# Recurrence of a streaming encoder on one core: each set of transposes placed behind a gate unit of its own

## What is computed

```python
p = hn @ w_in                                   # q, fp, vi, z: 8 heads x 128 columns each
f = lb + (1 - lb) * sigmoid(fp); q = silu(q); g = log(f); k = 1 - f; v = vi
b = cumsum(g)                                   # within a chunk
o = einsum(scores(q, k, b), v) + (q * exp(b)) @ S0
S = exp(b_last) * S0 + (k * exp(b_last - b)).T @ v
o = o * rsqrt(mean(o * o) + EPS) * gnorm        # per head
out = (o * silu(z)) @ w_out
```

## Time and profile before

| what | value |
|---|---|
| device time, median of 3 runs | 1507.84 us (1505.77 to 1508.29) |
| profiled execution, its own time | 1508.62 us |
| its span, first to last instruction | 1506.8 us |
| mean granted TensorE clock | 0.979 of full speed |
| busy share | PE 93%, PEld 81%, DVE 62%, ACT 43%, POOL 37% |

### The profile page before, as it was taken

The page is one execution under the profiler, slowest core; times in us unless marked ns, Lnnn a source line. Parts: engine busy times, 40 slices in busy tenths (PEclk is TensorE's granted clock), DMA queues, the critical chain, the costliest instruction groups (busy, mean ns, idle before and its releaser), DMA issues. The chain is left out here.

```text
span 1506.8 us, 21428 instructions
## 1 busy us (share of the span) xinstructions
PE 1404.7 (93%) x8109; PEld 1220.5 (81%) x8109; DVE 933.7 (62%) x1765; ACT 643.4 (43%) x1136; POOL 559.2 (37%) x402
## 2 busy tenths in 40 slices
PE   4999999999996899999988999999999999998898
PEld 3999746999995455548878998989999999997786
DVE  7111388787793989744556676667676757576333
ACT  6233464677664555541122625243434343443121
POOL 4276501265553001100012646465555556464000
PEclk9999999999998999999998999999999999999899
DMA  6112100232312410001231101010101111105221
GB/s 223 29 43 57 28 1 15 72 87 75 96 48 67 140 29 15 4 24 63 100 88 43 43 20 57 20 57 20 57 27 50 35 43 34 43 6 201 99 85 63
DMA packets 96181, 86.79 MB, mean 58 GB/s; under 512 B 4528, under 2 KB 84272, under 8 KB 96080
## 3 DMA queue, kind: packets, MB, share of 16 engines
q1 hardware_dynamic: 94448, 80.60, 17.3%
q0 software_dynamic: 1632, 4.82, 0.9%
HBM read 65.43 MB, written 19.97 MB: 57 GB/s over the span
## 5 line engine op out<-in xcount | busy, mean ns | idle before, releaser
L186 PE MATMUL bank<-hn_hi,rw_hi 128*128 128x352 f32 x768 | 250.8, 327 | 1.5 <-PEq L1059 1.5
L186 PE MATMUL bank<-hn_hi,rw_lo 128*128 128x352 f32 x768 | 247.6, 322 | 0.0
L186 PE MATMUL bank<-hn_lo,rw_hi 128*128 128x352 f32 x768 | 247.3, 322 | 0.0
L186 PE MATMUL bank<-hn_hi,w_hi 128*128 128x352 f32 x672 | 218.9, 326 | 3.6 <-PEq L274 3.6
L186 PE MATMUL bank<-hn_lo,w_hi 128*128 128x352 f32 x672 | 216.4, 322 | 0.0
L186 PE MATMUL bank<-hn_hi,w_lo 128*128 128x352 f32 x672 | 216.2, 322 | 0.0
L186 PEld LDWEIGHTS bank<-hn_hi,rw_hi 128*128 128x128 f32 x768 | 144.9, 189 | 3.4 <-issue 3.0
L186 PEld LDWEIGHTS bank<-hn_lo,rw_hi 128*128 128x128 f32 x768 | 145.3, 189 | 0.0
L186 PEld LDWEIGHTS bank<-hn_hi,rw_lo 128*128 128x128 f32 x768 | 144.9, 189 | 0.0
L186 PEld LDWEIGHTS bank<-hn_hi,w_hi 128*128 128x128 f32 x672 | 126.9, 189 | 4.3 <-issue 3.7
L186 PEld LDWEIGHTS bank<-hn_lo,w_hi 128*128 128x128 f32 x672 | 127.2, 189 | 0.0
(11 more groups left out here) (233 smaller groups left out, 2950.5 us busy)
## 6 DMA issues: line engine op xcount, KB each, us to landing
rw_raw<-in_rec_w_in SPq DMA_DIRECT2D x32, 512.0 KB, 4.0
w_raw<-in_att_w_in SPq DMA_DIRECT2D x30, 512.0 KB, 4.0
q_rotated<-relu SPq DMA_DIRECT2D x24, 176.0 KB, 1.9
xin<-in_x_prompt SPq DMA_DIRECT2D x8, 512.0 KB, 4.1
q_tile<-q_rotated SPq DMA_DIRECT2D x8, 512.0 KB, 3.7
wo_raw<-in_att_w_out SPq DMA_DIRECT2D x4, 1024.0 KB, 10.0
x_again<-in_x_prompt SPq DMA_DIRECT2D x8, 512.0 KB, 4.1
residual<-h_rows SPq DMA_DIRECT2D x8, 512.0 KB, 2.9
```

What stands on the lines that cost most here:

```text
L186: last = pe.matmul(out, l, r, start=n == 0, stop=n == len(passes) - 1)
```

## The change

The value transposes of a head stood behind its value units (unit 8), and the output transposes of the head before and the key transposes together behind unit 11. Now the value transposes stand behind unit 9, the output transposes of the head before behind unit 10, the key transposes behind unit 11. On ACT the read of unit 9 stands ahead of the copy of the value transposes, with its wait for `zT` to be free. No instruction is added or taken away, and no other engine's list changes.

```diff
@@ PE, loop over heads p @@
                 for j in range(3, 9):
                     project(u + j)
+                project(u + 9)
                 for g in range(3):
                     multiply("v_T", p, g)
-                for j in range(9, 12):
-                    project(u + j)
+                project(u + 10)
                 if p:
                     for g in range(3):
                         multiply("out_T", p - 1, g)
+                project(u + 11)
                 for g in range(3):
                     multiply("k_T", p, g)
@@ ACT, loop over heads p @@
                 for j in range(5, 9):
                     decay(p, j)
+                if p >= 2:
+                    act.wait_ge(dve_read, n_dve[at["out_T", p - 2, 2, None] + 1])
+                read_projection(u + 9)
                 for g in range(3):
                     read_product("v_T", p, g, v[:, p % 2])
-                if p >= 2:
-                    act.wait_ge(dve_read, n_dve[at["out_T", p - 2, 2, None] + 1])
-                for j in range(9, 12):
+                for j in range(10, 12):
                     read_projection(u + j)
                 split(4 * p + 3 + SLOTS)
```

## The result

The changed kernel takes 1514.43 us in the median of 5 runs (1513.08 to 1515.18), the kernel before 1508.29 us beside it (1505.77 to 1509.12). The ratio is 1.0043, with a 95% interval of 1.0028 to 1.0058: slower by 6.1 us, where I had forecast a gain of 1.5 us that one could hardly have measured. The profiled execution took 1515.18 us, its span is 1513.4 us, and the mean granted clock 0.974 instead of 0.979.

A forecast was written before the change was run, and what follows sets the result against it. The prediction took DVE's own chain, through its gate to the key transposes, as the bound, with PE only having slack. Terms of -1.2, -0.3 and 0 gave -1.5 us, from 1507.84 to 1506.3 us; range 1502.5 to 1510.5.

The forecast's parts named there:

- Step (1): Value transposes (L1371): with unit 9 ahead of them, PE's 1.27 us wait for ACT's read of unit 8 goes.
- Step (3): ACT's value copies: table load and unit 9's read now come first, so copies start at 1138.26 instead of 1136.59.
- Step (4): PE in head 4: a new 2.5 us wait before output group 1; heads 1 to 6 gain 0.
- the pin: Second key transpose group: reuses an output transpose bank, so it waits for DVE's gate, unmoved, at 1144.05 in head 4.
- the slack: Head 4, second key group: PE would arrive 0.25 us before DVE's gate lets it start.
- The value taken, 0: Heads 1 to 6: the change in time put into the forecast, neither gain nor loss.
- the bound of +0.2: Heads 1 to 6: loss per head if ACT's copy or signal takes 0.3 us more, 1.2 us in all.
- (5): Head 0: no output transposes, so nothing of DVE's holds its keys; it gains 1.2 us.
- (6): Head 7: the gate starts at 1363.24 instead of 1363.50, a gain of 0.3 us, bounds 0 and 0.8.
- Step (7): Unit 11 ends 2.2 us later; weight load, ACT's cast and key copies slip as much, under cover, costing 0.
- The sum: Whole kernel: -1.2 us for head 0, -0.3 for head 7 and 0 elsewhere, -1.5 us.
- rival B: Clock falls behind the single 2.5 us wait in heads 1 to 6: 6 to 12 us less 1.5, 1512 to 1518; chance 0.08.

## Why the prediction was wrong

**Step (1), right.** No PE wait on ACT is left at L1371; unit 9 covers the read.

**Step (3) and (4), right in size.** The new wait was forecast at the second output group, on ACT's copy, six times and some 2.3 us each; it is 13.6 us in six, 2.3 each.

**Step (4), the pin, right; the slack, just used up.** Head 1 is the one head without a fall of the clock. Before the change, unit 0 of the next head starts behind the key transposes 1.67 us after the gate does (first two lines); after it 1.68 (last two), although no wait is left ahead of the keys:

```profile
921.22 1.55 DVE L1610 SCALAR_TENSOR_TENSOR g_head<-wide,columns,gate_rec 128x512 f32<-128x512 f32 x3
922.89 0.40 PE L186 MATMUL bank<-hn_hi,rw_hi 128*128 128x352 f32 x1
...
919.88 1.56 DVE L1612 SCALAR_TENSOR_TENSOR g_head<-wide,columns,gate_rec 128x512 f32<-128x512 f32 x3
921.56 0.40 PE L186 MATMUL bank<-hn_hi,rw_hi 128*128 128x352 f32 x1
```

PE comes to the pin just as it opens. The 0.25 us to spare were used up, since from the end of the wait to the keys PE takes 4.68 us and not the 4.44 put (1138.96 to 1143.4), and the head costs nothing: 73.92 us from states to states, against 73.94. The value taken, 0, was right, and the bound of +0.2 was not needed. With 20 transposes in the place of the wait, heads 1 to 6 take 444.0 us against 443.8, and the whole is worth -1.4 us, against -1.5.

**Steps (5) and (6), right in size.** Head 0: from the end of unit 8 to the states it takes 25.0 us (834.17 to 859.17) instead of 26.2 (834.32 to 860.49), 1.2 less, as forecast. Head 7 gave 0.2 in the same stretch (15.66 us instead of 15.86; 0.3 forecast). Its gate moved by less than 0.1 (13.97 us behind unit 8 instead of 14.03), so the way in which the 0.2 came about is not shown.

**Step (7), right.** Unit 11's later end cost nothing: with the clock up, no wait appears behind it.

**The clock, the step that failed.** The sum put nothing for the clock behind the new wait. The mechanism was on the list as rival B, with its place and its price: 6 to 12 us less 1.5, or 1512 to 1518. The trace has 8.2 us in heads 1 to 6 (859.17 to 1311.20, against 860.49 to 1304.27), or 1.2 to 1.4 in each of four heads and 2.9 in one. Less the 1.4 of heads 0 and 7 that is some 6.8; the medians differ by 6.1, and the time is 1514.4. What failed is its chance, 0.08, and with it the forecast and the range, which left B out. I had two rows, a clock that held behind an idle time of 1.81 us and one that fell behind 3.43, and a new wait of 2.5 between them. The one argument against B was that PE is dense on both sides. The rows did not support it, for PE was just as dense ahead of the 3.43 us (window of the kernel before):

```profile
168.00:170.00 2.00, 2.00 (x18) 1.78 (x17) 0.00 (x0) 0.41 (x1) 2.00 (x2) 1.00 0.00 0
```

Between ends that differ by 10 us for the kernel, with nothing to tell them apart, the chances should have been near even, and the range should have reached to 1518. The Trainium skill, TensorE: Matmul & The Clock Gate, section Why this matters for your kernels, warns of idle gaps between bursts of matmuls only from a length above the 2.5 us forecast here. Read with that limit it is not contradicted by the 1.81 us row, and by its number it spoke against B. The measurement decides: these runs show the fall already behind 2.1 to 2.4 us of idle time, in 5 of 6 heads.

A sentence of the prediction holds the other half of the lesson: PE has 1.27 + 1.29 us of slack. The change hardly shortened that slack, it put it in one piece.

## What to carry to other kernels

When a wait is only slack against another engine's loop, moving work in front of it moves the idle time; look for the bank or buffer that ties the two and change the order of reuse, which here was worth 1.2%. Two short waits can be cheaper for PE than one long one, so a reordering that merges them has to be priced at the lower clock. To test for a clock effect, put useless matmuls into the wait: if the kernel gets faster with more work and the granted clock stays up, it was the clock.

## What the runs showed of the hardware

- The granted clock of PE held behind idle times of 1.3 to 1.6 us (six of six, with 8 added transposes) and of 1.5 to 1.8 (three of three, with ACT's part undone). It fell behind 2.1 to 2.4 us in 10 of 12 heads of the change's two traces; the two heads in which it held had waits of 2.34 and 2.36 us, no shorter than the others, so the length alone does not decide at this size. In the windows one fall costs 1.5 us, in two of the ten 2.9.
- 20 transposes in the place of the wait kept the clock at 1.00 in all six heads, in two traces.
- In these stretches 1.00 is 2.4 GHz, with 0.16 us from matmul to matmul, and at 1.2 GHz (0.50) it is 0.29.
- DVE and POOL hold each other up: a norm of 1.42 or 4.22 us, a weight split of 4.5 or 2.4 us, the one long where the other is short. It moves DVE's gate by 2 us in single heads, more than most of what was argued about here. The recorded starts do not tell which of the two will stand.
